# Norm statistics from products of sixteen equal columns, with root and reciprocal on four columns spread back by matmuls

## What is computed

```python
def rms_norm(t, w):
    tf = t.astype(jnp.float32)
    y = tf * lax.rsqrt(jnp.mean(tf * tf, axis=-1, keepdims=True) + NORM_EPS)
    return (y * w.astype(jnp.float32)).astype(t.dtype)

def modulate(h, shift, scale):
    return h * (1.0 + scale[:, None, :]) + shift[:, None, :]
```

## Time and profile before

| | |
|---|---|
| median of 3 runs | 4035.22 us |
| lowest and highest | 4031.64 and 4037.05 us |
| profiled execution, whole | 4035.21 us |
| its span | 4033.4 us |
| TensorE busy | 3567.5 us, 88% |
| VectorE busy | 1873.4 us, 46% |
| ScalarE busy | 1103.7 us, 27% |
| mean granted TensorE clock | 0.938 of full speed |

### The profile page before, as it was taken

The page is one execution under the profiler, slowest core; times in us unless marked ns, Lnnn a source line. Parts: engine busy times, 40 slices in busy tenths (PEclk is TensorE's granted clock), DMA queues, the critical chain, the costliest instruction groups (busy, mean ns, idle before and its releaser), DMA issues. The chain is left out here.

```text
span 4033.4 us, 36059 instructions
## 1 busy us (share of the span) xinstructions
PE 3567.5 (88%) x12706; PEld 2407.5 (60%) x12706; DVE 1873.4 (46%) x2537; ACT 1103.7 (27%) x1425; POOL 111.7 (3%) x204
## 2 busy tenths in 40 slices
PE   4997789999689999867999997999979679989987
PEld 1444468877358877633788643588847346558433
DVE  5856256536358835142664297466233433153001
ACT  1221243323432213321453201344142222132000
POOL 0000000000000000000000300000000000000000
PEclk9896999999899999978999998999989889999988
DMA  5231146522035522201233210233322112223111
GB/s 215 99 120 54 42 148 196 190 89 73 11 110 192 195 86 84 63 0 52 80 97 94 73 52 32 78 96 94 97 94 84 32 52 84 83 68 98 48 62 62
DMA packets 100408, 360.87 MB, mean 89 GB/s; under 512 B 11152, under 2 KB 11168, under 8 KB 100064
## 3 DMA queue, kind: packets, MB, share of 16 engines
q1 hardware_dynamic: 77936, 276.07, 21.5%
q0 software_dynamic: 20080, 75.27, 5.8%
q10 hardware_dynamic: 2304, 8.39, 0.5%
HBM read 357.59 MB, written 2.10 MB: 89 GB/s over the span
## 5 line engine op out<-in xcount | busy, mean ns | idle before, releaser
L1613 DVE TENSOR_TENSOR weight_lo<-weight_ring,weight_hi 128x1024 fp32r<-128x1024 f32 (+1 forms) x390 | 468.6, 1203 | 930.0 <-ACT weight_hi L1124 926.2
L1124 ACT ACTIVATE weight_hi<-weight_ring 128x1024 fp32r<-128x1024 f32 (+1 forms) x390 | 406.3, 1043 | 1266.2 <-PE proj_banks L688 927.6
L688 PE MATMUL proj_banks<-h_hi,weight_hi 128*128 128x512 f32 x1584 | 617.3, 390 | 9.6 <-DVE weight_lo L1613 9.6
L688 PE MATMUL proj_banks<-h_hi,weight_lo 128*128 128x512 f32 x1584 | 617.0, 390 | 0.0
L688 PE MATMUL proj_banks<-h_lo,weight_hi 128*128 128x512 f32 x1584 | 616.8, 389 | 0.0
L1647 DVE RECIPROCAL scratch<-scratch 128x512 f32<-128x512 f32 (+1 forms) x39 | 129.2, 3312 | 479.4 <-ACT scratch L1124 479.3
L688 PEld LDWEIGHTS proj_banks<-h_hi,weight_hi 128*128 128x128 f32 x1584 | 297.7, 188 | 73.4 <-issue 11.6
L688 PEld LDWEIGHTS proj_banks<-h_hi,weight_lo 128*128 128x128 f32 x1584 | 297.6, 188 | 62.2
L688 PEld LDWEIGHTS proj_banks<-h_lo,weight_hi 128*128 128x128 f32 x1584 | 297.7, 188 | 61.4
L645 PE MATMUL proj_banks<-scratch,weight_ring 128*128 128x512 f32 x640 | 293.5, 622 | 27.5 <-DMA weight_ring<-in_w_dnr 27.5
L688 PE MATMUL proj_banks<-mid_hi,weight_hi 128*128 128x512 f32 x704 | 275.3, 391 | 7.3 <-DVE weight_lo L1613 7.3
(11 more groups left out here) (259 smaller groups left out, 4378.6 us busy)
## 6 DMA issues: line engine op xcount, KB each, us to landing
weight_ring<-in_w_up SPq DMA_DIRECT2D x176, 512.0 KB, 3.6
ada_ring<-in_ada POOLq DMA_DIRECT2D x96, 512.0 KB, 3.9
weight_ring<-in_w_dn SPq DMA_DIRECT2D x64, 512.0 KB, 3.5
weight_ring<-in_w_br SPq DMA_DIRECT2D x32, 512.0 KB, 3.7
weight_ring<-in_w_upr SPq DMA_DIRECT2D x32, 512.0 KB, 3.6
weight_ring<-in_w_dnr SPq DMA_DIRECT2D x32, 512.0 KB, 4.5
scratch<-in_ada POOLq DMA_DIRECT2D x24, 512.0 KB, 4.3
weight_ring<-in_w_dn SPq DMA_DIRECT2D x32, 384.0 KB, 3.1
```

The costliest lines, as they stand in the source:

```text
L688: last = mm(proj.banks[:, u % RING, :], stationary(split0 + n)[:, w], moving(k), start=k + m == 0, stop=k == kt - 1 and m == 2)
L1124: return nc.scalar.activation(out, in_, func, **kw)
L1613: return v.tensor_tensor(out, a, b, op)
```

## The change

The sum of squares changes its form. VectorE adds the squares of tiles 0 to 6 elementwise into the first of them (`sum_up`), in `residual` where a residual comes before the norm, and at the start of `norm` for norms 0, 9 and 10. TensorE then uses the squares as the stationary operand, 128 tokens at a time, against sixteen columns of ones: four products for the sum and four for the last square, which leave the sums with tokens on partitions, in sixteen equal columns for each block of tokens. ScalarE takes the root of one column of each, 128x4, and VectorE the reciprocal of 128x4. Four more products, each with a column broadcast to 128 as the stationary operand and the identity as the moving one, put the result back into a 128x512 bank (new keys "bc"), which VectorE reads from PSUM in its multiplications.

Steps are folded: VectorE multiplies by the gain and the reciprocal root in one instruction, ScalarE adds the shift and rounds in one, VectorE forms lo as (H + shift) - hi. A root of a constant column after the seventh square brings the table in.

Steps are reordered: the roundings of a down projection alternate with the squares (`round_down` goes), the two first chunks of the next stage are rounded before the last square and after the root, and in `first_pair` the lo products run over k outside and over the two tiles inside.

```diff
@@ mixing_keys @@
-    k = [("ss", 0)]
+    k = [("ss", 0), ("bc", 0)]
...
@@ tensor_program, first_pair @@
-        for t in range(2):
-            for k in range(KD):
-                if t == 0:
-                    pe.wait_ge(s["h_ready"], h_count(r, k))
+        for k in range(KD):
+            pe.wait_ge(s["h_ready"], h_count(r, k))
+            for t in range(2):
                 last = mm(proj.bank((name, t)), c.hi(split0 + t)[:, k * P:(k + 1) * P], lo(k), start=False, stop=k == KD - 1)
-            last.then_inc(proj.full_sem, 1)
+                if k == KD - 1:
+                    last.then_inc(proj.full_sem, 1)
...
@@ tensor_program, norm @@
-        sum_squares(("ss", r), lambda k: (s["sq_ready"], 8 * r + k + 1), lambda k: T(squares_at(r) + k), KD)
+
+        bank = open_bank(mix, ("ss", r))
+        for half, (sem, n) in enumerate(((s["sq_summed"], 6 * (r + 1)), (s["sq_ready"], 8 * (r + 1)))):
+            pe.wait_ge(sem, n)
+            for j in range(NB):
+                squares = T(squares_at(r) + (KD - 1 if half else 0))
+                last = mm(bank[:, j * SUMS:(j + 1) * SUMS], squares[:, j * P:(j + 1) * P], c.square("ones")[:, 0:SUMS], start=half + j == 0, stop=half + j == NB,
+                          skip_group_check=True)
+        last.then_inc(mix.full_sem, 1)
+        bank = open_bank(mix, ("bc", r))
+        pe.wait_ge(s["rstd_ready"], r + 1)
+        for j in range(NB):
+            last = mm(bank[:, j * P:(j + 1) * P], c.small[:, INV + j:INV + j + 1].broadcast_to([P, P]), c.square("ident"), start=True, stop=True)
+        last.then_inc(mix.full_sem, 1)
...
@@ scalar_program, round_down (its calls in swiglu and conv_ffn go too) and norm @@
-    def round_down(layer):
-
-        for n in range(SPLIT_RING, 3 * KD):
-            round_chunk(f"dn{layer}", n)
-
     def norm(r):
 
         for k in range(KD):
             if r == 0:
                 act.wait_ge(s["x_loaded"], 16)
             elif r in NORM_AFTER:
-                act.wait_ge(*proj.emptied((NORM_AFTER[r], k)))
+                stage = NORM_AFTER[r]
+                if stage in SPLIT:
+                    for n in range(3 * k + SPLIT_RING, min(3 * k + 3 + SPLIT_RING, 3 * KD - 1)):
+                        round_chunk(stage, n)
+                act.wait_ge(*proj.emptied((stage, k)))
             else:
                 act.wait_ge(s["x_ready"], 8 * (r - 9) + k + 1)
             st.done(f(T(squares_at(r) + k), X(k), ACT.Square), s["sq_ready"])
-            if r in SPLIT_UP and k == KD - 2:
-
-                up = SPLIT_UP[r]
-                for n in range(SPLIT_RING):
-                    round_chunk(up, n)
-        root(("ss", r), T(RSTD), D)
+            if k == KD - 2:
+
+                st.link(f(c.small[:, STD:STD + 1], eps, ACT.Sqrt))
+                if NORM_AFTER.get(r) in SPLIT:
+                    round_chunk(NORM_AFTER[r], 3 * KD - 1)
+                if r in SPLIT_UP:
+                    round_chunk(SPLIT_UP[r], 0)
+        act.wait_ge(*mix.filled(("ss", r)))
+        ins = f(c.small[:, STD:STD + NB], mix.bank(("ss", r))[:, 0:NB * SUMS:SUMS], ACT.Sqrt, scale=1.0 / D, bias=eps)
+        ins.then_inc(mix.emptied(("ss", r))[0], 1)
+        if r in SPLIT_UP:
+            round_chunk(SPLIT_UP[r], 1)
         if r in MODULATED:
             use, layer, part, ready = MODULATED[r]
             act.wait_ge(s["mod_ready"], ready)
             for k in range(KD):
                 act.wait_ge(s["xn_ready"], 8 * list(MODULATED).index(r) + k + 1)
-                ins = f(H(k), H(k), ACT.Identity, scale=c.g(use, k), bias=c.m(layer, part, k))
-                ins.then_inc(s["h_raw"] if r in SPLIT_NORMS else s["h_ready"], 1)
                 if r in SPLIT_NORMS:
-                    round_h(r, k)
+                    st.done(f(c.norm_hi(r, k), H(k), ACT.Identity, bias=c.m(layer, part, k)), s["h_rounded"])
+                else:
+                    f(H(k), H(k), ACT.Identity, bias=c.m(layer, part, k)).then_inc(s["h_ready"], 1)
         elif r in SPLIT_NORMS:
...
@@ vector_program, sum_up, norm, residual @@
+    def sum_up(r, k):
+
+        total = T(squares_at(r))
+        dve.wait_ge(s["sq_ready"], 8 * r + k + 1)
+        st.done(tt(total, total, T(squares_at(r) + k), ALU.add), s["sq_summed"])
+
     def norm(r):
+        if r not in NORM_AFTER:
+            for k in range(1, KD - 1):
+                sum_up(r, k)
         if r in SPLIT_UP:
-            for n in range(SPLIT_RING):
-                rest_chunk(SPLIT_UP[r], n)
-        inverse(("ss", r), T(RSTD))
+            rest_chunk(SPLIT_UP[r], 0)
+        dve.wait_ge(*mix.emptied(("ss", r)))
+        st.done(v.reciprocal(small[:, INV:INV + NB], small[:, STD:STD + NB]), s["rstd_ready"])
+        if r in SPLIT_UP:
+            rest_chunk(SPLIT_UP[r], 1)
+        dve.wait_ge(*mix.filled(("bc", r)))
+        rstd = mix.bank(("bc", r))
         for k in range(KD):
             if r in MODULATED:
-                st.done(tt(H(k), X(k), T(RSTD), ALU.mult), s["xn_ready"])
+                ins = stt(H(k), X(k), c.g(MODULATED[r][0], k), rstd, ALU.mult, ALU.mult)
+                st.done(ins, s["xn_ready"])
             else:
                 name, at = PLAIN[r]
                 out = X(k) if r == 8 else H(k)
-                ins = stt(out, X(k), c.v(name, at + k), T(RSTD), ALU.mult, ALU.mult)
+                ins = stt(out, X(k), c.v(name, at + k), rstd, ALU.mult, ALU.mult)
                 if r == 8:
                     st.done(ins, s["x_ready"])
                 elif r in SPLIT_NORMS:
-                    ins.then_inc(s["h_raw"], 1)
+                    st.done(ins, s["h_raw"])
                 else:
                     ins.then_inc(s["h_ready"], 1)
                     dve.wait_ge(s["h_ready"], h_count(r, k))
+        dve.sem_inc(*mix_release(mix, ("bc", r)))
         if r in SPLIT_NORMS:
             for k in range(KD):
                 dve.wait_ge(s["h_rounded"], 8 * SPLIT_NORMS.index(r) + k + 1)
-                tt(c.norm_lo(r, k), H(k), c.norm_hi(r, k).bitcast(F32), ALU.subtract).then_inc(s["h_ready"], 1)
+                hi = c.norm_hi(r, k).bitcast(F32)
+                if r in MODULATED:
+                    use, layer, part, _ = MODULATED[r]
+                    ins = stt(c.norm_lo(r, k), H(k), c.m(layer, part, k), hi, ALU.add, ALU.subtract)
+                else:
+                    ins = tt(c.norm_lo(r, k), H(k), hi, ALU.subtract)
+                ins.then_inc(s["h_ready"], 1)
                 dve.wait_ge(s["h_ready"], h_count(r, k))
...
+        after = [r for r in NORM_AFTER if NORM_AFTER[r] == stage][0]
         for k in range(KD):
             key = (stage, k)
             if stage in SPLIT:
                 for n in range(3 * k + 2, min(3 * k + 5, 3 * KD)):
                     rest_chunk(stage, n)
+            if k >= 2:
+                sum_up(after, k - 1)
             dve.wait_ge(*proj.filled(key))
```

21 lines of the change are left out of this document (11 added, 10 removed).

## The result

The changed kernel takes **4044.5 us** (median of 12 runs, 4036.9 to 4052.2) against 4035.5 (12 runs of the kernel before, beside it). The ratio is 1.0021, with a 95% interval of 1.0013 to 1.0029. It is a little slower, outside the range of 3976 to 4020, where 3999.5 was predicted. The profiled execution has a span of 4038.9 us.

What follows compares the result with a forecast made beforehand. TensorE, busy 3567.5 of 4033.4 us, was taken as the bound, with time to win only where it idles or runs slowly. Terms 33.1 + 7.3 + 4.3 - 6 - 3 = 35.7 off 4035.2 gave 3999.5 us, range 3976 to 4020.

Steps and rivals of the forecast that it cites:

- stalls in the down projections: Rival: roundings alternating with squares stall the weights, 2 us at each of 28 boundaries, giving 4055 us; chance 4%.
- the slow products that the prediction priced behind a pair: After TensorE's longer idle at norms, eight products at the lower clock cost 0.2 each, 1.6 us; 0.8 at norms 2 and 4.
- spreading products at the lower clock: Products putting the reciprocal back into a bank may partly run at 1.2 GHz: 0.3 us off each norm, 1.8 in all.
- The pairs: First two tiles behind a norm: TensorE sets the pace, 12.55 us against 15.41 at norm 1, 2.85 sooner.
- The wait behind the pair: TensorE's idle time after a norm's first two tiles grows from 2.05 to 3.6 us; 1.6 lost at six norms.
- Norm 0: Six uncovered VectorE additions, then small products on a cold TensorE, delay the first product: loss 6 us, 3.5 at full clock.
- a sign of being wrong: One of the listed observations that would refute the forecast: small instructions above 0.2 us each.
- The new order of the lo products: In a norm's first two tiles, chunk 2's rounding and a table load lose cover: 1.6 us lost at six norms.
- The rival that was built on the drain: At seven removed table loads, the skill's 2.66 us a switch would bring some 10 us more, 3990 us; chance 5%.

## Why the prediction was wrong, point by point

**The term that failed isn't in the sum.** The prediction begins with "the span can shrink only where TensorE stands still or runs slowly", and takes the time of the products that keep TensorE busy as given. It goes through what the change removes, adds and moves, and passes over the line that widens "small": that it shifts every h tile against the weights was put at nothing, without a reason. The runs show that it makes 9168 products some 0.006 us longer each. It cost 45 us when put into the kernel before, and 50.7 when taken out of the changed one, more than the 42 of the whole rest. Neither did a rival cover it: the slower side was given to stalls in the down projections, 4%. They didn't come: the idle time ahead of the products of "dn", in the changed kernel at the old width, is 7.3 us in all, as in the kernel before.

```profile
L694 PE MATMUL proj_banks<-mid_hi,weight_hi 128*128 128x512 f32 x704 | 275.4, 391 | 7.3 <-DVE weight_lo L1634 7.3
```

**The terms that were in the sum came close together, in part by luck.** They are read in the changed kernel at the old width, as its lead over the kernel before at the same instruction; a term is the difference of two leads. The rows end at the start of tile 2, so the slow products that the prediction priced behind a pair stand in the row after it, in both columns.

| stretch, by its last instruction (before; changed at the old width) | lead, us | term | predicted |
|---|---|---|---|
| norm 0 to the idle time of 11 us (397.05; 403.90) | -6.9 | -6.9 | -6 |
| to tile 2 behind norm 1 (538.94; 537.55) | 1.4 | 8.2 | 8.8 |
| norm 2 (919.11; 909.01) | 10.1 | 8.7 | 7.25 |
| norm 3 (1175.70; 1154.87) | 20.8 | 10.7 | 8.05 |
| "up1", "dn1", norm 4 (1562.81; 1536.03) | 26.8 | 6.0 | 5.4 |
| to the start of the products ahead of norm 5 (1849.9; 1826.6) | 23.3 | -3.5 | -0.8 |
| norm 5 (1935.67; 1909.27) | 26.4 | 3.1 | 4.1 |
| "up2", "dn2" (2283.95; 2260.08) | 23.9 | -2.5 | -1.6 |
| norm 6 (2297.45; 2266.66) | 30.8 | 6.9 | 7.3 |
| to tile 2 behind norm 7 (2587.07; 2548.10) | 39.0 | 8.2 | 5.3 |
| to "rk", norms 8 and 9 (3016.54; 2973.53) | 43.0 | 4.0 | 2.7 |
| norm 10 (3578.69; 3537.26) | 41.4 | -1.6 | -3 |
| end (span 4033.4; 3993.0) | 40.4 | -1.0 | 0 |

The predicted terms add up to 37.5, and to 35.7 with the 1.8 taken off for spreading products at the lower clock. Three rows are off by more than 2 us: norm 3, the stretch behind norm 4, and norm 7, whose term includes 2.6 won between norm 6 and the depthwise stage behind it. Each trace is one execution, which matters most at the first row. The kernel with the old order has the same program up to that instruction and is only 2.4 us late there (399.43), and the changed kernel itself, which differs by the width alone, 2.0 (399.07); that this row agrees with the 6 is luck.

Three mechanisms inside the rows came out otherwise. *The pairs* take 13.5, 13.0 and 12.9 us at norms 1 to 3, where 12.55 was predicted, and at norms 4, 5 and 7, where no change was priced, they went from 12.6, 12.9 and 13.3 to 14.0, 14.0 and 13.5. Together the six are 4.6 us longer than the prediction has them. *The wait behind the pair* grew by 1.6 at five of the six norms and by nothing at norm 3. *The slow products behind it* came at norms 4, 5 and 7 (1.5, 2.5 and 1.6 us) and not at norms 1 and 2, and at norm 3 the ones of the kernel before went: 4.0 more in all, where 6.4 were priced. So more was lost in the pairs and less behind them, and the sum came near. One small item can be seen: at norm 1 the spreading products were at full clock (1.13 for eight), at norm 6 not:

```profile
2263.61 2.05 PE L770 MATMUL mix_banks<-squares,small 128*128 128x128 f32 x8 [0.79 <-DVE small L1683]
```

**Norm 0**, predicted with a loss of 6: the first product came at 72.45 in the changed kernel against 66.66, 5.8 later, and the small products took 3.57 and 2.05 where 4.4 and 2.5 were priced. At 0.22 and 0.26 an instruction they are above the 0.2 that the prediction named as a sign of being wrong. **The new order of the lo products** costs 1.4, 1.6 and 1.6 up to tile 2 at norms 1, 5 and 7, as said; norm 3 pays nothing and norm 4 pays 2.5, where 1.6 was put on each.

**The table load.** ScalarE with work right ahead of it, in the changed kernel behind norm 1:

```profile
530.27 1.06 ACT L1143 ACTIVATE weight_hi<-weight_ring 128x1024 fp32r<-128x1024 f32 x1
531.35 1.28 ACT L1143 ACT_TABLE_LOAD   x1
532.64 0.60 ACT L1143 ACTIVATE scratch<-proj_banks 128x512 f32<-128x512 f32 x1
```

The load begins 0.02 us after the rounding ends and the next step 0.01 after the load: 1.28 us a switch, though the engine was busy right before it. The Trainium skill, "ScalarE: Activation LUTs", section "What ACT_TABLE_LOAD costs", adds a drain of 1.38 to it. No row here has it, beside an idle engine or a busy one: in the changed kernel 123 of the 124 loads with a step behind them have it start 0.011 to 0.013 us after they end, and the last one waits for something else. The loads are not fewer either, 125 in both kernels: that of norm 1 has moved from behind the sums (513.75 in the earlier trace rows) to 503.47, ahead of the last square. The rival that was built on the drain had no ground.

## What to carry to other kernels

Every new or wider tensor moves all that is allocated behind it, so put new ones last or use free columns, and read the time from start to start of the main product in a stretch away from the edit, before and after: a count of 442 against 430 in 100 us at the same clock finds in one line what no chain of waits shows. Keep the split operands that TensorE reads together, the next weights among them, at distances of a whole multiple of 256 bytes, until a run of your own says otherwise. And where an edit moves work under another engine's cover, apply it only where that cover exists: the same additions that VectorE makes beside a residual take 4.3 us of their own at norms 0 and 10.

## What the runs showed of the hardware that was not expected

- The time of a split product of 512 columns depends on where its operands lie: 0.2267 us at distances that are multiples of 256 bytes, 0.2289 to 0.2333 at 32, 64, 128, 192 and 224 bytes off, at the same granted clock. One weight tensor off its place also slows the products beside which it is loaded, though they don't read it (232.5 against 226.5 ns). The fp32 products of 512 columns take 0.429 us at full clock wherever the h tiles stand.
- At a granted clock of 0.50 an instruction with 16 columns takes 0.216 us (64 of them at norm 9, back to back for 13.8 us, through which the clock stayed at 0.50); at a clock of 1.00 it takes 0.12 (0.96 for eight). One of 512 columns takes 0.44 at full clock (7.03 for sixteen). So the cost of a small product is hardly its columns.
- The length of a wait alone doesn't tell the clock behind it. After 3.63 to 3.64 us without work TensorE ran on at full clock at norm 1, at half the clock for twelve products at norm 5, and at norm 7 for six products at full clock and then eight at half (0.60 to 0.63 us each). After 2.05 us it stayed at full clock at norm 7, and ran at half for eight and nine products at norms 1 and 5 of the kernel with the old order.
